# A decoder step on one core: the normalised token tiles split one round earlier, and one tile fewer turned ahead of the first products

## The reference, cut to what matters

```python
def rms_norm(x, g):
    xf = x.astype(jnp.float32)
    y = xf * lax.rsqrt(jnp.mean(xf * xf, axis=-1, keepdims=True) + EPS)
    return (y * g.astype(jnp.float32)).astype(x.dtype)
...
    y, st_new = hybrid_mixer(rms_norm(x, norm_mix), lw, st)     # x: 1024 + 64 tokens x 1024
    # hybrid_mixer begins with
    proj = h @ w_in                                             # w_in: 1024 x D_IN
```

## Time and profile before

| | |
|---|---|
| median of 3 runs | 2216.6 us |
| profiled execution | 2216.44 us, its span 2214.6 us |
| PE busy | 2188.7 us, 99% of the span |
| DVE, ACT, POOL busy | 1109.8, 656.8, 1091.8 us |

### The profile page before, as it was taken

One profiled execution on the slowest core, in us unless ns is written; L12 is line 12 of the kernel. 1 busy time (PEld: TensorE's weight loads), 2 busy tenths in 40 slices (PEclk: granted clock), 3 DMA queues, 4 the chain that ended last, 5 costly groups with the idle time before them and its releaser, 6 DMA issues. The chain is left out here.

```text
span 2214.6 us, 33494 instructions
## 1 busy us (share of the span) xinstructions
PE 2188.7 (99%) x13547; PEld 2072.7 (94%) x13547; DVE 1109.8 (50%) x1746; ACT 656.8 (30%) x1155; POOL 1091.8 (49%) x1363
## 2 busy tenths in 40 slices
PE   7999999999999999999999999999999999999998
PEld 6999999999999999999999999889989899899897
DVE  7522221799754535543442466555464463643615
ACT  5444442333321111232222112133223232232332
POOL 3544444677343233222235564517485575764851
PEclk9999999999999999999999999999999999999999
DMA  5333332112121111222234555301211202102022
GB/s 162 107 103 100 98 107 74 48 49 69 53 89 51 40 50 50 60 60 80 89 120 139 170 182 171 102 11 48 76 29 49 66 12 77 58 20 77 20 67 81
DMA packets 172925, 172.31 MB, mean 78 GB/s; under 512 B 6706, under 2 KB 147318, under 8 KB 172763
## 3 DMA queue, kind: packets, MB, share of 16 engines
q1 hardware_dynamic: 170177, 160.20, 23.5%
q0 software_dynamic: 2304, 8.91, 1.1%
q10 hardware_dynamic: 290, 1.05, 0.2%
HBM read 135.62 MB, written 34.89 MB: 77 GB/s over the span
## 5 line engine op out<-in xcount | busy, mean ns | idle before, releaser
L966 PE MATMUL acc<-h_hi,w_hi 128*128 128x368 f32 (+2 forms) x2040 | 669.9, 328 | 2.4 <-POOL w_lo L1939 1.9
L968 PE MATMUL acc<-h_hi,w_lo 128*128 128x368 f32 (+2 forms) x2040 | 663.8, 325 | 0.0
L967 PE MATMUL acc<-h_lo,w_hi 128*128 128x368 f32 (+2 forms) x2040 | 663.2, 325 | 0.0
L1939 POOL TENSOR_TENSOR w_lo<-w_raw,w_hi 128x256 fp32r<-128x256 f32 x508 | 380.5, 778 | 471.3 <-ACT w_hi L1463 471.3
L966 PEld LDWEIGHTS acc<-h_hi,w_hi 128*128 128x128 f32 x2040 | 383.5, 188 | 7.9 <-issue 4.0
L967 PEld LDWEIGHTS acc<-h_lo,w_hi 128*128 128x128 f32 x2040 | 383.6, 188 | 0.2
L968 PEld LDWEIGHTS acc<-h_hi,w_lo 128*128 128x128 f32 x2040 | 383.6, 188 | 0.0
L1463 ACT ACTIVATE w_hi<-w_raw 128x1024 fp32r<-128x1024 f32 (+2 forms) x145 | 138.7, 957 | 359.7 <-PE acc L968 184.0
L2292 DVE TENSOR_TENSOR x<-pz,x 128x512 f32<-128x512 f32 x214 | 144.2, 687 | 91.0 <-PE pz L968 88.4
L1939 POOL TENSOR_TENSOR a_op<-a_raw,a_op 128x256 fp32r<-128x256 f32 x196 | 159.4, 846 | 22.4 <-DVE a_raw L2292 16.6
L2292 DVE TENSOR_TENSOR a_raw<-acc,a_raw 128x368 f32<-128x368 f32 (+1 forms) x112 | 44.7, 420 | 208.2 <-ACT a_raw L1825 118.8
(11 more groups left out here) (524 smaller groups left out, 4706.9 us busy)
## 6 DMA issues: line engine op xcount, KB each, us to landing
w_raw<-in_w_in SPq DMA_DIRECT2D x70, 512.0 KB, 4.0
w_raw<-in_w_up SPq DMA_DIRECT2D x32, 512.0 KB, 4.2
gate_values<-staging SPq DMA_DIRECT2D x29, 544.0 KB, 3.7
gsig<-gate_values SPq DMA_DIRECT2D x29, 544.0 KB, 3.7
w_raw<-in_w_down SPq DMA_DIRECT2D x18, 512.0 KB, 3.5
b_raw<-branch_outputs POOLq DMA_DIRECT2D x16, 544.0 KB, 5.5
w_raw<-in_w_branch SPq DMA_DIRECT2D x16, 512.0 KB, 4.8
g_raw<-in_w_in SPq DMA_DIRECT2D x14, 512.0 KB, 5.1
```

What stands on the lines that cost most here:

```text
L966: pe.matmul(out, lh, rh, start=first, stop=False, skip_group_check=more)
L967: pe.matmul(out, lh, rl, start=False, stop=False, skip_group_check=more)
L968: return pe.matmul(out, ll, rh, start=False, stop=last, skip_group_check=more)
L1939: return pool.tensor_tensor(out, x, y, op)
```

## The change

- ACT: the high half of a tile is written in the round i-2 and not i-3: high 0 follows square 2, not square 3. The split of a weight unit stands ahead of the square of its round, not behind it.
- DVE: low i-2 in place of low i-3. Mean 0 stands ahead of the copies of the gain, and mean 1 behind scaling 0.
- POOL: the four quarters of a unit's low half are cut in two pairs, one ahead of root 4 (or 7), one ahead of root 5 (or 8), where all four stood behind root 4 (or 7).
- PE: four tiles are turned ahead of the first product, not five. Turns 4 to 7 alternate with the half products, and turn 8 follows turn 7.
- The identity for the turns is fetched by ACT's queue behind the gain, not by SP's behind the first tile.

The diff, cut to its core:

```diff
@@ SP
             for i in range(NT + 1):
                 sp.dma_start(xin[0:rows_of[i], i, :], x_tiles[i]).then_inc(x_in[i], 16)
-                if i == 0:
-                    sp.dma_start(ident, a["con"][:, C_ID:C_ID + P]).then_inc(con_in, 16)
@@ PE
-            for i in range(NT - 3):
+            for i in range(NT - 4):
                 turn_tokens(i)
             for i in range(4):
                 for q in range(2):
                     early(i // 2, 0, 2 * (i % 2) + q)
-                turn_tokens(NT - 3 + i)
+                turn_tokens(NT - 4 + i)
+            turn_tokens(NT)
             turn_params()
@@ ACT
             act.dma_start(gain_r[:, :], a["norm_mix"]).then_inc(sem("gain_in"), 16)
-            for i in range(NT + 4):
+            act.dma_start(ident, a["con"][:, C_ID:C_ID + P]).then_inc(con_in, 16)
+            for i in range(NT + 3):
+                if i in (4, 7):
+                    split_hi(i // 3 - 1)
                 if i <= NT:
                     n = rows_of[i]
                     act.wait_ge(x_in[i], 16)
...
-                if i in (4, 7):
-                    split_hi(i // 3 - 1)
-                if i >= 3:
-                    t0, t1 = TT_[i - 3]
+                if i >= 2:
+                    t0, t1 = TT_[i - 2]
                     for hh in range(2):
-                        act.wait_ge(sem("rows_to_turned"), 2 * (i - 3) + hh + 1)
-                        copy(h_hi[:, 4 * hh:4 * hh + 4, t0:t1], turned_x(i - 3, hh)).then_inc(sem("rows_to_hi"), 1)
+                        act.wait_ge(sem("rows_to_turned"), 2 * (i - 2) + hh + 1)
+                        copy(h_hi[:, 4 * hh:4 * hh + 4, t0:t1], turned_x(i - 2, hh)).then_inc(sem("rows_to_hi"), 1)
@@ POOL
+            def first_lo(u, quarters):
+                pool.wait_ge(hi_ready, u + 1)
+                for q in quarters:
+                    c0, c1 = q * UNIT // 4, (q + 1) * UNIT // 4
+                    ins = tt(w_lo[:, u, c0:c1], w_raw[:, u, c0:c1], w_hi[:, u, c0:c1].bitcast(F32), ALU.subtract)
+                if quarters[-1] == 3:
+                    ins.then_inc(w_ready, 1)
+
             for i in range(NT + 1):
+                if i in (4, 7):
+                    first_lo(i // 3 - 1, (0, 1))
+                if i in (5, 8):
+                    first_lo(i // 3 - 1, (2, 3))
                 n = rows_of[i]
                 pool.wait_ge(sem("row_ms"), i + 1)
                 tt(rs[0:n, i:i + 1], ss[0:n, i:i + 1], mhalf[0:n, i:i + 1], ALU.pow).then_inc(sem("row_rs"), 1)
-                if i in (4, 7):
...
@@ DVE
+            first_mean(0)
             dve.wait_ge(sem("gain_spread"), 1)
             for j in range(2):
                 ins = dve.tensor_copy(gain_x[:, j * 512:(j + 1) * 512], pz[:, 3 + j, :])
             link(ins)
-            for i in range(NT + 4):
-                if i <= NT:
...
+            for i in range(NT + 3):
+                if 2 <= i <= NT:
+                    first_mean(i)
                 if 1 <= i <= NT + 1:
...
+                if i == 1:
+                    first_mean(1)
-                if i >= 3:
-                    t0, t1 = TT_[i - 3]
+                if i >= 2:
+                    t0, t1 = TT_[i - 2]
```

More of the change, by code:

```diff
@@ L2302, in params_out, with first_mean @@
                 tt(lbt[:, 0, :], lbl, lbl, ALU.subtract).then_inc(sem("lb_diff"), 1)
+            def first_mean(i):
+                n = rows_of[i]
+                dve.wait_ge(sem("row_sq"), i + 1)
+                dve.tensor_scalar(ss[0:n, i:i + 1], ss[0:n, i:i + 1], 1.0 / D, EPS, ALU.mult, ALU.add) \
+                    .then_inc(sem("row_ms"), 1)
+            first_mean(0)
             dve.wait_ge(sem("gain_spread"), 1)
@@ L2321, in _ @@
                         .then_inc(sem("rows_scaled"), 1)
-                if i >= 3:
-                    t0, t1 = TT_[i - 3]
+                if i == 1:
+                    first_mean(1)
+                if i >= 2:
+                    t0, t1 = TT_[i - 2]
                     for hh in range(2):
-                        dve.wait_ge(sem("rows_to_hi"), 2 * (i - 3) + hh + 1)
-                        tt(h_lo[:, 4 * hh:4 * hh + 4, t0:t1], turned_x(i - 3, hh),
+                        dve.wait_ge(sem("rows_to_hi"), 2 * (i - 2) + hh + 1)
+                        tt(h_lo[:, 4 * hh:4 * hh + 4, t0:t1], turned_x(i - 2, hh),
                            h_hi[:, 4 * hh:4 * hh + 4, t0:t1].bitcast(F32), ALU.subtract).then_inc(sem("rows_to_lo"), 1)
```

## The result

The changed kernel takes 2220.32 us (median of 20 runs, 2215.33 to 2221.46); before took 2215.22 (20 runs, 2214.00 to 2217.29). The ratio is 1.0019, 95% interval 1.0013 to 1.0025: slower by 5.1 us by the medians and by 4.2 (2.9 to 5.5) by the ratio, where +1.4 was forecast. The profiled execution took 2221.43 us, its span is 2219.6 us, 5.0 more than before.

A forecast was written before the change was run, and what follows sets the result against it. PE was taken as the bound, busy 2188.7 of 2214.6 us. The first gate's gain is lost by the second, DVE ends the phase 1.4 us later, and this carries through: 2216.6 becomes 2218.0 us, range 2214.5 to 2221.0.

The forecast's parts named there:

- rival B: At the first products: PE is still at the low pace, slowing half a product and turn 4; +4.3 us, 2220.9; chance 0.14.
- DVE's end of the phase: DVE's last work of the start phase, the parameters' copy at 35.39 us and next phase at 36.27; forecast 1.4 later.
- PE's wait near 75 us: PE's next real wait after the start phase, ending at 75.74 us; forecast to end 1.4 later and last 0.5 longer.
- Rival C: In DVE's 39 us after the start phase: the late end is absorbed, no change, 2216.6 us; chance 0.13.
- second gate: Start of PE's product with weight unit 1, at 28.73 us before; forecast at 28.7, the early gain gone.
- first gate: Start of PE's first product, at 20.63 us before; forecast at 19.6, 1.0 us earlier.
- the products at half pace: Sign at PE's first products: if they start at half pace, the forecast of +1.4 us is wrong.
- the wait of 3.2 us: PE's wait ahead of unit 1's product, at the second gate; forecast to be 3.2 us, not 1.86.
- Bound of 0.2%: On the whole time: a change under 0.2%, or 4.4 us, can hardly be told from none; chance of same 0.90.

## Why the prediction was right or wrong, point by point

- *The number.* The time of 2220.3 lies inside the range of 2214.5 to 2221.0, and that is in part luck. The sum stood on 2216.6, the median of three executions; twenty put before at 2215.2. As a difference the forecast was +1.4, rival B +4.3, and measured are 5.1: counted from 2215.2 the range would have ended at 2219.6, below the result. The case that was forecast can have occurred in four executions of twenty at most.
- *What carries.* Right. DVE's end of the phase moved by 5.11 us, PE's wait near 75 us by 5.12, the span by 5.0. In all other profiles the first two move alike to 0.02 us, and the medians follow within 0.8 us in nine of the eleven kernels, 1.2 and 1.6 in the other two. Rival C, that DVE absorbs it, is out. The wait at that place did not grow by 0.5 as forecast (0.65 us, not 0.63): PE lost the half microsecond earlier, at 56 us, in a wait of 0.52 for DVE that was not there before.
- *The order of ACT, DVE and POOL.* Right in its sequence. The changed kernel's profile has scaling 3 at 16.43 (16.3 forecast), roots 4 and 7 at 1.53 us each (about 1.5), the first product at 19.69 (19.6).
- *The size of the order's cost.* With the clock kept up, DVE ended the phase 0.66 later, not 1.4. The missing 0.7 is, as far as can be told, the identity's edit, which I took at 0 (0 to -0.45): it brings tile 2 in 1.4 us earlier, and in the kernel before it is worth 0.64 on DVE. Order alone is then about +1.3, an estimate from these two (0.66 and 0.64). The part behind the second gate was well sized: in the kernel with all idle work the parameters were turned 6.51 us behind it and copied 8.12 behind it, against 6.5 and 8.0. In the profiled execution of the change the gain arrived late (its product began at 3.18 us, not 2.22), which cost that back, since scaling 0 now waits for the gain alone: the first gate was hit by two errors that met. The kernel with idle work ahead of turns 2 and 3 shows it with quick turns: gain at 3.12, first product at 19.65; with all idle work 2.20 and 18.71. The kernel before with PE's new order had 3.16 too, and the one with the identity alone 2.21, so this is not the identity's doing. Of the twelve profiled kernels four had 2.2 and eight 3.0 to 3.3; what decides it is open.
- *Which case.* Wrong. The forecast was the case without a slow clock, at 0.60, and rival B had 0.14. Sixteen of twenty executions were 3 to 6 us above before, and the one profiled had the products at half pace, which the prediction itself named as a sign that its forecast is wrong. The sentence that failed is the one against B, "PE works as many us from 8.8 to 16 as it did from 10.3 to 16". It counted the work and not the holes: turn 2 was quick, as after the same work before, and the clock fell behind it, in the hole of 2.00 us ahead of turn 3. In three variants (PE's order undone, unit 1 earlier, POOL's order undone) turns 2 and 3 were slow from the start on, with holes of 1.0 to 1.2 us between them. So the low pace at the products comes in two ways; which of them the other fifteen of the sixteen executions had is not known.
- *The price of B.* 2.9 us was set for one slow half product and turn 4. Against the kernel with all idle work, whose phase ends 4.45 earlier on DVE (36.93 and 41.38), it comes apart like this: 0.98 by the gain, up to the first gate (19.69 and 18.71); 1.94 from the first gate to the second (11.15 and 9.21), most of it the half product (3.85 and 2.12); 1.53 behind the second gate (10.54 and 9.01). So the clock, which the forecast had at nothing, cost 3.5 us in these profiles. The last part was not in B: I had named the wait of 3.2 us there and not asked what the clock does in it. The medians part by 3.9 us, by 4.4 as distances from before. One profiled execution stands on each side, and that with idle work (2215.12 us) was the second fastest of its eleven.
- *Bound of 0.2%.* The ratio's interval, 1.0013 to 1.0025, lies on both sides of it. The loss is resolved by 20 runs all the same, so the chance of 0.90 for "within 0.2%" was more than the cases carried, with B at its edge.
- *The Trainium skill.* Its sentence that the number of slow matmuls differs from run to run (TensorE: Matmul & The Clock Gate, "What's actually happening") is borne out: behind the same order and the same waits turn 2 took 1.10 us in the profile of the changed kernel and 1.97 in that with unit 1 earlier. What I drew from it was only the favourable side, quick turns 0 and 1, which no profile here shows. A spread from 2215.3 to 2221.5 over twenty executions is what it meant for this kernel.

## What to carry to other kernels

Ahead of the first long run of matmuls, list PE's holes and not only their sum: in the profiled execution the products behind holes of 2.0 and 3.2 us ran at half pace, and sixteen of twenty executions took 3 to 6 us more than before. Then ask what stands behind the slow stretch: the same pace cost little where nothing on the chain waited for it. When a unit of work is moved behind another in an in-order queue, ask where the next unit stands: with the clock kept up the first gate came 1.9 us sooner and the second only 0.8, and in the changed kernel as it ran the second came 2.1 us later, because its input stood behind the very step that had been moved. And a shift of a phase's end is worth what the engine that is full afterwards makes of it, which one row of busy times shows.

## What the runs showed of the hardware that was not expected

- One fetch of 64 KB less between tile 0 and tile 1 on SP's queue, moved to ACT's, brought tiles 1 and 2 in 1.3 to 1.8 us earlier (5.8 to 6.2 and 7.2 to 7.5 us in the nine kernels with it, 7.5 to 7.7 and 8.8 to 8.95 in the three without). One issue takes 0.42 us; the rest is not explained.
- Between 17 and 24 us PE of the changed kernel was busy 6.09 of 7.00 us at a granted clock of 0.51; before it was busy 5.28 at 1.00 and did 38 matmuls, not 23. A busy share in the profile says nothing of the pace.
- In three kernels (PE's order undone, unit 1 earlier, POOL's order undone) the views read a clock of 1.00 while turns 2 and 3 took 1.97 us, as every profile here does for the slow turns 0 and 1. The first record of the clock in these three traces is the rise, at 21.5 to 27.9 us; ahead of it the clock is not known, a mean clock of 0.999 doesn't exclude a slow start, and the pace of equal matmuls is what tells.
